# Multilayer blocks: three input quarters of the MLP's down product by 26 block products, the last by sevens

## The reference, cut to what matters

```
D_MODEL, SEQ, D_FF = 1024, 512, 4096

def sq_relu_mlp(h, w1, w2):
    return jnp.square(jax.nn.relu(h @ w1)) @ w2

for layer in range(2):
    x = x + mixer(rms_norm(x, mix_norm[layer]))        # RG-LRU, then forgetting attention
    x = x + sq_relu_mlp(rms_norm(x, mlp_norm[layer]), mlp_w1[layer], mlp_w2[layer])
```

## Time and profile before

| | us |
|---|---|
| median of 3 runs | 2904.4 (2902.56 to 2908.75) |
| the profiled execution | 2907.54 |
| its span, first to last instruction | 2905.8 |
| PE busy | 2852.3 (98%) |
| DVE busy | 1873.1 (64%) |
| ACT busy | 757.4 (26%) |
| POOL busy | 350.8 (12%) |
| granted TensorE clock | 0.997 of full speed, the upper of the two levels (2.4 GHz) |

### The profile page before, as it was taken

The page is one execution under the profiler, slowest core; times in us unless marked ns, Lnnn a source line. Parts: engine busy times, 40 slices in busy tenths (PEclk is TensorE's granted clock), DMA queues, the critical chain, the costliest instruction groups (busy, mean ns, idle before and its releaser), DMA issues.

```text
span 2905.8 us, 41791 instructions
## 1 busy us (share of the span) xinstructions
PE 2852.3 (98%) x17453; PEld 2429.7 (84%) x17453; DVE 1873.1 (64%) x2645; ACT 757.4 (26%) x1404; POOL 350.8 (12%) x374
## 2 busy tenths in 40 slices
PE   9999999999999999999999999999999999999999
PEld 8888888888678888878788888888888867888888
DVE  5577764566677764444676578887556434888753
ACT  1513410023622430011456522221010273211101
POOL 0312000220002000010033301111020021111101
PEclk9999999999999999999999999999999999999999
DMA  4222232222011323221100032223222200222321
GB/s 143 69 92 87 75 100 75 87 87 73 30 59 59 116 70 105 73 73 47 64 3 4 13 116 72 77 83 109 80 73 78 83 1 30 87 87 87 109 70 39
DMA packets 189478, 209.46 MB, mean 72 GB/s; under 512 B 9332, under 2 KB 182092, under 8 KB 189292
## 3 DMA queue, kind: packets, MB, share of 16 engines
q1 hardware_dynamic: 189100, 206.72, 22.1%
q10 hardware_dynamic: 192, 0.08, 0.0%
HBM read 204.65 MB, written 2.10 MB: 71 GB/s over the span
## 4 chain that ended last, share of the span: by engine, by line
PE 91%; DVE 5%; ACT 2%; issue 1%; POOL 0%; DVEq 0%; ACTq 0%; POOLq 0%
PE pp L277 56%; PE pp L493 9%; PE pp L151 8%; PE pp L275 3%; PE pp L3568 2%; PE pp L2786 1%; DVE arena L356 1%; PE pp L1930 1%; PE pp L2769 1%; PE pp L2351 1%; PE pp L3545 1%; PE pp L3602 1%; PE pp L2740 1%; PE pp L1954 1%; PE pp L3164 1%
## 5 line engine op out<-in xcount | busy, mean ns | idle before, releaser
L277 PE MATMUL pp<-arena 128*128 128x256 f32 (+2 forms) x7952 | 1741.1, 381 | 8.4 <-DVE arena L1568 2.2
L277 PEld LDWEIGHTS pp<-arena 128*128 128x128 f32 x7952 | 1506.6, 190 | 240.8 <-issue 5.8
L493 PE MATMUL pp<-arena 128*128 128x256 f32 x1248 | 269.7, 379 | 0.0
L493 PEld LDWEIGHTS pp<-arena 128*128 128x128 f32 x1248 | 236.7, 190 | 32.8
L151 PE MATMUL pp<-arena 128*128 128x256 f32 (+4 forms) x1056 | 238.2, 385 | 1.4 <-DVE arena L1294 1.4
L151 PEld LDWEIGHTS pp<-arena 128*128 128x128 f32 (+3 forms) x1056 | 194.3, 185 | 43.0 <-issue 5.2
L368 ACT COPY arena<-pp 128x512 f32<-128x512 f32 (+2 forms) x54 | 31.5, 583 | 676.7 <-PE pp L277 573.4
L1316 POOL TENSOR_TENSOR sq<-sq 128x512 f32<-128x512 f32 (+2 forms) x41 | 71.5, 1745 | 831.3 <-ACT sq L1307 828.3
L3322 ACT ACTIVATE arena<-arena,par 128x528 f32<-128x528 f32 (+1 forms) x88 | 67.7, 817 | 380.3 <-DVE arena L3354 380.3
L356 DVE TENSOR_TENSOR arena<-arena 128x256 f32<-128x256 f32 (+8 forms) x148 | 151.2, 1041 | 5.5 <-POOL arena L3398 2.4
L3398 POOL TENSOR_TENSOR arena<-arena 128x528 f32<-128x528 f32 (+1 forms) x44 | 70.8, 1609 | 488.9 <-DVE arena L3366 488.9
(11 more groups left out here) (418 smaller groups left out, 3114.5 us busy)
## 6 DMA issues: line engine op xcount, KB each, us to landing
arena<-in_ffn_up_dram SPq DMA_DIRECT2D x44, 1024.0 KB, 5.1
arena<-in_mlp_w_dram SPq DMA_DIRECT2D x40, 1024.0 KB, 6.5
arena<-in_mlp_w_dram SPq DMA_DIRECT2D x48, 512.0 KB, 4.4
arena<-in_ffn_down_dram SPq DMA_DIRECT2D x16, 1408.0 KB, 7.0
arena<-in_fox_w_in_dram SPq DMA_DIRECT2D x12, 1024.0 KB, 5.4
arena<-in_lru_w_in_dram SPq DMA_DIRECT2D x8, 1024.0 KB, 6.7
arena<-in_lru_w_out_dram SPq DMA_DIRECT2D x4, 1024.0 KB, 5.0
arena<-in_fox_w_out_dram SPq DMA_DIRECT2D x4, 1024.0 KB, 5.0
```

Of the source, the lines that this page charges most:

```text
L277: return pe.matmul(k.pp[seventh(k, name, n, i) % NB][:, j, 0:hw], stationary[i][:, kk, j * P:(j + 1) * P], moving[i][:, kk, :], start=kk = ...
L493: mm = pe.matmul(bank[:, j * GW:(j + 1) * GW], w[:, kk, j * P:(j + 1) * P], x[:, kk, :], start=first and j == 0 and kk == 0, stop=kk == 1, ...
```

## The change

The down product's first three input quarters (input tiles 0 to 7, 8 to 15, 16 to 23) become block products, quarters n = 3, 4, 5 of the same `Quarters`, and only the last 8 input tiles go by sevens (`down`), with input and weight sums of half the size. Each of the new quarters has inputs of its own, so 18 input sums are made for each (`sets`, numbers 1 to 3): six on DVE within the quarter before, handed to `quarters_sums` as `next_inputs`, twelve on POOL behind them. They overwrite the buffers of the set before, so each waits for the product that last read its buffer (`q.products.wait(e, n - 1, ...)`); x9 alternates between two buffers (`turns`). The kept blocks of quarters 3, 4 and 5 leave PSUM by ACT's Identity into three places; POOL adds the second to the first, and then, block by block (`GATHER`), adds the third, multiplies by the factor by token and adds to `x`: 8 and 24 operations. DVE's adds of the sevens wait for that count (`add_gathered`).

```
+    q = Quarters(k, rest, [(w1, 0, 2 * (NU + 2 * n) * GW) for n in range(NQ)] + [(w2, m * KT, 0) for m in range(ND)],
+                 [X] * NQ + [hid[:, m * KT:(m + 1) * KT, :] for m in range(ND)], [0] * NQ + [1 + m for m in range(ND)],
+                 inputs, turns, sums, temps)
+    plan_seven(k, down, w2, [(2 * n * GW + GW, 2 * n * GW) for n in range(2)], ND * KT, KT)
...
 def quarters_inputs(e, q, n, part):
...
+        q.input_sums.wait(e, m, 1)
+        if m:
+            q.products.wait(e, n - 1, 2)
+        e.tensor_tensor(x21, q.x(n, 0, 0), x9, ALU.subtract).then_inc(q.input_sums.sem, 1)
...
 def quarters_sums(e, q, n, more, inputs=None):
...
     e.tensor_tensor(s34, q.raw(n, 1, 3), s23, ALU.add).then_inc(q.sums.sem, 1)
     q.products.wait(e, n, 18)
+    if inputs:
+        inputs(e)
     e.tensor_tensor(s28, q.raw(n, 1, 2), s26, ALU.subtract).then_inc(q.sums.sem, 1)
...
         product_seven(e, k, up, X, Su, Tu, hw, ready, up_s)
-        for n in range(NQ):
+        for n in range(NQ + ND):
+            if n >= NQ:
+                e.wait_ge(squared, all_squared(n - NQ - 1))
             quarters_multiply(e, q, n)
-        q.left(e, NQ - 1, 0)
-        product_seven(e, k, downs[0], hid_a, Sd, Td, hw, ready_a, down_s, apart=True,
...
-        product_seven(e, k, downs[1], hid_b, Sd, Td, hw, ready_b, down_sb)
+        q.left(e, NQ + ND - 1, 0)
+        product_seven(e, k, down, hid_d, Sd, Td, hw, ready_down, down_s, apart=True,
+                      ahead={TWO: lambda: q.left(e, NQ + ND - 1, 1), SEVEN: lambda: q.left(e, NQ + ND - 1, 2),
+                             SIX: lambda: q.left(e, NQ + ND - 1, 3)})
...
     def keep(e, n, i, h, bank, sign):
-        return e.activation(block(n, i, h), tiled(bank), ACT.Relu, scale=sign)
+        if n < NQ:
+            return e.activation(block(n, i, h), tiled(bank), ACT.Relu, scale=sign)
+        o = total(i, h) if n == NQ else part(n - NQ, i, h)
+        return e.activation(o, tiled(bank), ACT.Identity, scale=sign)
...
+        for m in range(ND):
+            e.wait_ge(squared, all_squared(m - 1))
+            q.input_sums.wait(e, m + 1, 6)
+            for i in range(1, 3):
+                quarters_inputs(e, q, NQ + m, i)
+            if m >= 2:
+                for j, (i, h) in enumerate(KEPT):
+                    q.kept.wait(e, NQ + m - 1, j + 1)
+                    step(e.tensor_tensor(total(i, h), total(i, h), part(m - 1, i, h), ALU.add))
+        for i, h in GATHER:
+            q.kept.wait(e, NQ + ND - 1, KEPT.index((i, h)) + 1)
+            step(e.tensor_tensor(total(i, h), total(i, h), part(ND - 1, i, h), ALU.add))
+            step(e.tensor_tensor(total(i, h), total(i, h), by_token(k, (i, h), hw), ALU.mult))
+            x = k.x[:, 2 * i:2 * i + 2, t0 + h * hw:t0 + (h + 1) * hw]
+            step(e.tensor_tensor(x, x, total(i, h), ALU.add))
```

## The result

The changed kernel takes 2930.1 us (median of 4 runs, 2928.1 to 2930.8), the kernel before 2905.8 (4 runs, 2902.6 to 2908.8): ratio 1.0079, 95% interval 1.0066 to 1.0092. The profiled execution took 2928.09 us with a span of 2926.4, against 2905.8: 20.6 us more. The forecast was 2922, range 2904 to 2940, slower with 0.78.

A forecast was written before the change was run, and what follows sets the result against it. TensorE, busy for 98% of the span, was taken as the bound. Terms gave +7.9 us a layer, 15.8 for two, plus 1.1: +17 on the 2904.4 median, 2921.4, rounded up to 2922 with wake-ups; range 2904 to 2940.

The forecast's parts named there:

- The matmuls that go: Down product: 48 records fewer a layer at 0.216 us each, -10.4 us a layer.
- The transitions: Three changes of quarter a layer: GpSimd's input sums slow DVE's weight sums, 2.4 us each, +7.2 a layer.
- The bill for s16: At a change of quarter, PE's wait for the weight sum the third product reads: 4.4 - 0.15 - 2.5 = 1.75 us.
- the further 0.45 for s22 and the wake-ups: At a change of quarter, the fifth product's weight sum raises the bill to 2.2 us, wake-ups to 2.4.
- every hit costs a whole GpSimd sum: At a change of quarter, six hits of 1.17 us, 7.0 in place of 4.4, making the transition 5.0.
- Quarter 5: GpSimd's eight sums of kept parts meet about eight DVE weight sums in the last block quarter: +3.0 us a layer.
- The drain of the banks: After the last block quarter, the first seven waits for ACT's eviction of kept block 6: +2.6 us a layer.
- SIX against the gather: In the sevens, PE waits for DVE's eight input sums, slowed by GpSimd's gather: +6.2 us a layer.
- The second group of sevens: PE waits there for DVE's weight sums beside GpSimd's sums of squares in the first layer: 1.1 us, once.
- company costs nothing: Rival: GpSimd's sums fall into DVE's moves and idle time; the two layers save 17 us, 2887 us; chance 0.12.
- Only the tail pays: Rival: transitions absorbed, bank drain and the eight sums against the gather stay; -2.3 us a layer, 2900 us; chance 0.08.
- Every sum pays in full: Rival: all upper bounds come true, 17.9 us a layer, 2942 us in total; chance 0.15.

The follow-up runs named there:

- e1_short_sums: Changed kernel with GpSimd's twelve input sums of each of quarters 3 to 5 cut to one column: 2911.4 us.
- e5_parity: Changed kernel with the two orders of the banks swapped, so the banks the sevens want first are free early; nothing left out: 2930.2 us.
- e4_short_gather: Changed kernel with the 24 gathering steps of a layer on GpSimd cut to one column: 2916.3 us.
- e2_writes: Changed kernel with each of GpSimd's input sums in quarters 3 to 5 replaced by two writes of the same size: 2908.3 us.
- e7_late: Changed kernel with GpSimd's last nine input sums of a quarter waiting for that quarter's eighth weight sum: 2912.2 us.
- e8_all: Changed kernel with late GpSimd sums, swapped banks, the sevens' four long input sums made earlier and an eight-addition gather: 2895.3 us, 0.9962 of the kernel before.

## Why the prediction was right, and where it was not

Right were the sign, the mechanism and most single waits; the sum was low by 4 us against the spans (17 forecast, 20.6) and by 7 against the medians (24.4), within the range.

- **The matmuls that go**: 848 records of each layer's down product, 96 fewer in all, L277 with 6608, as counted. The block products are listed as 2464 of L497 and 32 that read x9 from `sq`.
- **The transitions**: forecast 2.4 us, measured 1.65 to 1.72 in waits. Six sums were hit, as I took it, for 5.1 us instead of 4.4. The bill for s16, 1.75, is near what came, but for other readers. s16 lands at 381.58, 1.9 us after the time at which an unstopped PE would want it (376.22 + 2 x 1.73 = 379.68); PE never waits for it, because it has paid before, ahead of the first product for kept block 4 and ahead of the second for s36 (L694), two waits that I did not price. What did not come is the further 0.45 for s22 and the wake-ups, and PE does not idle over five products but over two. Eight moves stand between s28 and s16, not seven. By the clock of the whole quarter, records against time, a transition still costs 2.6 us (from 377.08 - 0.86 = 376.22 to 424.58 - 0.80 = 423.78 are 47.56 us for 208 records that took 44.97): the records around the stops make up for it. The alternative that I weighed, that every hit costs a whole GpSimd sum (5.0 a transition), did not come: four of the six hits cost 0.95 to 1.09 us and two 0.46 and 0.47, 5.1 / 6 = 0.85 on average.
- **Quarter 5**: forecast 3.0, measured 2.18 and 2.19 as a wait. The cause that I gave (the eight sums meet eight weight sums) is half of it: e1_short_sums has them in full, beside the same weight sums, and no wait. It needs the lateness that DVE brings from the twelve sums before. The two terms are not independent.
- **The drain of the banks**: forecast 2.6, measured 2.68. But as an added term it was wrong: e5_parity takes it away and gains nothing. Of the 2.6 + 6.2 the true reading is one wait for DVE's eight sums, 8.8 us in all, of which the first part is spent ahead of ONE.
- **SIX against the gather**: forecast 6.2, measured 6.21 in the first layer, 4.83 in the second, where the 48 records before it took 11.98 us instead of 10.4 at a granted clock below 1 and so used up part of the same wait. Eight sums in 16.3 us, forecast 16.2; e4_short_gather confirms the cause. The gather had four of its groups left then, not five, which was still enough to stand beside all eight sums.
- **The second group of sevens**: forecast 1.1, measured 0.16.
- **What failed: no term for the matmuls behind a wait.** I priced each wait at its own length. Behind it the matmuls ran slower: 3.6 us in the first layer with the clock granted at 0.84 and 0.96, and some 3 us more around the stops. This is the difference of the first layer, 11.7 instead of 7.9, once the smaller waits are set against it (16.2 instead of 19.0). That these two misses point opposite ways, -2.8 and +6.6, is luck, and it brought the sum as near as it is.

The rivals: "company costs nothing" is out by the timeline of DVE and by e1_short_sums. "Only the tail pays" is what remains when the transitions are freed: I had given it 2900, and e1_short_sums, e2_writes and e7_late put it at 2908 to 2912. The tail's slower matmuls come on top, then the wait for GpSimd ahead of the stage behind the second layer, and in e1_short_sums 3 us between the layers, where nothing is edited. "Every sum pays in full" (2942) had the waits too long: they stayed below the forecast's, 16.2 us a layer against 19.0, and what carried the time above the forecast were the slower matmuls.

## What to carry to other kernels

Handing sums with two SBUF inputs to GpSimd beside VectorE's own sums of that kind spared VectorE nearly nothing here (41 of 50 us came back), so place them beside work that reads PSUM (the moves stayed at 0.69 us; no run tried this place by itself), or where the consumer has a lead, as nine of them waiting for eight weight sums did for 18 us. Two waits that end at the same late event are one term: price the event, not each wait. And to each new wait of a full TensorE add what the matmuls behind it lose.

## What the runs showed of the hardware that was not expected

- GpSimd's writes do not hold VectorE up: 0.68 us a sum beside writes of 0.53, 1.75 beside sums that read.
- Waits of 2.2 to 6.2 us in a stream of matmuls were followed by stretches with a granted clock below 1, and not always. Behind 2.18 us in quarter 5 the clock was 0.84 for 11 us in the first layer, behind 2.19 it was 1.00 in the second. Behind the same wait of 2.68 us the 48 records took 10.60 us at 1.00 in the first layer of the changed kernel, 11.98 at 0.88 in its second, 12.28 at 0.86 in the first of e1_short_sums. What decides between them stays open; no run here was made for it. Waits of 0.8 us were followed by a clock of 1.00, and so were those of 1.51 and 1.92 us in the first layer of e8_all.
